# Gate products of 32 rows, two at a time on two groups of partitions, in a hybrid encoder trunk

## What is computed

```python
g_f = (jax.nn.log_sigmoid((a_f @ w2_f + b_f).astype(jnp.float32)) / GLA_TAU).reshape(B, S, GLA_HEADS, GLA_DK)
g_b = (jax.nn.log_sigmoid((a_b @ w2_b + b_b).astype(jnp.float32)) / GLA_TAU).reshape(B, S, GLA_HEADS, GLA_DK)
...
b = jnp.cumsum(gc, axis=2)
```

## Time and profile before

| | us |
|---|---|
| median of 3 runs | 2955.53 |
| fastest, slowest run | 2954.26, 2968.17 |
| the profiled execution's own time | 2966.03 |
| its span in the trace | 2964.2 |
| TensorE busy in it | 2886.0 |

### The profile page before, as it was taken

One profiled execution on the slowest core, in us unless ns is written; L12 is line 12 of the kernel. 1 busy time (PEld: TensorE's weight loads), 2 busy tenths in 40 slices (PEclk: granted clock), 3 DMA queues, 4 the chain that ended last, 5 costly groups with the idle time before them and its releaser, 6 DMA issues.

```text
span 2964.2 us, 48975 instructions
## 1 busy us (share of the span) xinstructions
PE 2886.0 (97%) x16038; PEld 2405.6 (81%) x16038; DVE 1605.5 (54%) x2745; ACT 1365.5 (46%) x2458; POOL 1143.6 (39%) x1118
## 2 busy tenths in 40 slices
PE   7999999999999999999999999999999999999998
PEld 6768888788788888887877888888887888888887
DVE  6577777766677777774435222254557554532111
ACT  4642255566555555553236111265657665632111
POOL 1211111356233333332331762087766767623221
PEclk9999999988999999999999999999999999999999
DMA  7243355586211111113653332242235233244321
GB/s 281 68 123 103 106 165 163 166 284 211 59 57 57 57 57 57 57 57 115 200 180 121 135 149 89 96 132 100 99 103 181 101 106 101 96 164 149 101 98 57
DMA packets 277929, 355.56 MB, mean 120 GB/s; under 512 B 21604, under 2 KB 185572, under 8 KB 277255
## 3 DMA queue, kind: packets, MB, share of 16 engines
q1 hardware_dynamic: 272424, 338.14, 35.0%
q0 software_dynamic: 3072, 11.54, 1.0%
q10 hardware_dynamic: 2304, 4.20, 0.4%
HBM read 241.99 MB, written 111.80 MB: 119 GB/s over the span
## 4 chain that ended last, share of the span: by engine, by line
PE 84%; DVE 4%; issue 4%; ACT 4%; POOL 2%; DMA 2%; SPq 0%; DVEq 0%; ACTq 0%; POOLq 0%
PE PS L3025 6%; PE PS L3029 6%; PE PS L3033 6%; PE PS L366 4%; PE PS L2384 4%; PE PS L2385 4%; PE PS L2386 4%; PE PS L368 4%; PE PS L367 4%; PE PS L1805 4%; PE PS L1783 4%; PE PS L2552 4%; PE PS L2553 3%; PE PS L2554 3%; PE PS L1806 2%
## 5 line engine op out<-in xcount | busy, mean ns | idle before, releaser
L366 PE MATMUL PS<-hTh,whi 128*128 128x512 f32 x640 | 257.8, 403 | 1.5 <-DVE hTl L320 1.1
L3025 PE MATMUL PS<-hTh,wc 128*128 128x512 f32 x896 | 244.3, 395 | 6.6 <-DVE zu L2959 5.0
L368 PE MATMUL PS<-hTh,wlo 128*128 128x512 f32 x640 | 250.5, 391 | 0.0
L367 PE MATMUL PS<-hTl,whi 128*128 128x512 f32 x640 | 250.3, 391 | 0.0
L2781 POOL TENSOR_TENSOR wc<-wpr,wc 128x512 fp32r<-128x512 f32 x128 | 177.1, 1383 | 180.9 <-ACT wc L2777 180.9
L1886 ACT ACTIVATE pb__160<-PS,nm,rq 128x512 f32<-128x512 f32 x256 | 197.3, 779 | 106.7 <-DVE nm L1949 106.5
L3029 PE MATMUL PS<-hTh,wc 128*128 128x512 f32 x896 | 240.4, 390 | 0.0
L3033 PE MATMUL PS<-hTl,wc 128*128 128x512 f32 x896 | 240.4, 390 | 0.0
L2384 PE MATMUL PS<-ow_h,of_h 128*128 128x512 f32 x576 | 224.4, 390 | 1.8 <-DVE oy L2335 1.8
L2386 PE MATMUL PS<-ow_h,of_l 128*128 128x512 f32 x576 | 224.1, 389 | 0.0
L2385 PE MATMUL PS<-ow_l,of_h 128*128 128x512 f32 x576 | 224.1, 389 | 0.0
(11 more groups left out here) (309 smaller groups left out, 7130.1 us busy)
## 6 DMA issues: line engine op xcount, KB each, us to landing
wpr<-wuz SPq DMA_DIRECT2D x128, 256.0 KB, 3.2
xt<-x SPq DMA_DIRECT2D x8, 2048.0 KB, 9.0
mw<-wmod SPq DMA_DIRECT2D x64, 256.0 KB, 2.7
oxt<-x SPq DMA_DIRECT2D x32, 512.0 KB, 4.6
sg_v<-vev SPq DMA_DIRECT2D x64, 256.0 KB, 2.4
vm<-sg_v SPq DMA_DIRECT2D x32, 512.0 KB, 3.9
sgT<-mT SPq DMA_DIRECT2D x32, 512.0 KB, 3.5
chnk<-pev SPq DMA_DIRECT2D x48, 256.0 KB, 2.7
```

The lines of the kernel that those rows point to most:

```text
L366: pe.matmul(PS[:, bank, :], w[1][:, s, k, :], hTh[:, k, b], start=(k == 0), stop=False)
L367: pe.matmul(PS[:, bank, :], w[1][:, s, k, :], hTl[:, k, b], start=False, stop=False)
L368: mm = pe.matmul(PS[:, bank, :], w[2][:, s, k, :], hTh[:, k, b], start=False, stop=(k == KD - 1))
L3025: pe.matmul(o, wc[:, k, 0, kk, :], h_tile(hTh, k, kk), start=(kk == 0 and not onto), stop=False, skip_group_check=onto)
```

## The change

The 32 rows of `ga` and `gw2` are now held on two groups of partitions, 0 to 31 and 32 to 63. `gw2` is loaded twice, once to each group. `ga` is split by the parity of the block of positions: even blocks (tb = 0 and 2) on the first group, odd ones (tb = 1 and 3) on the second, so that it has 64 partitions with half as many columns. The first product of a pair reads from the first group, the second from the second. Banks, sums, and all that follows are as before. Two more DMAs are waited for, so the counts go from 80 to 112.

```diff
-        ga = at("ga", X0 + 24 * K, [2 * RANK, S])
+        ga = at("ga", X0 + 24 * K, [4 * RANK, 2, 512])
+        GROUP = (slice(0, 2 * RANK), slice(2 * RANK, 4 * RANK))
...
-        gw2 = at("gw2", X0 + 38 * K, [2 * RANK, 4 * P])
+        gw2 = at("gw2", X0 + 38 * K, [4 * RANK, 4 * P])
...
-            for dst, src in ((gw2[:, :], a["w2"]), (gb2[:, :], a["b2"]), (ggn[:, :], a["gnorm"]),
+            for dst, src in ((gw2[GROUP[0], :], a["w2"]), (gw2[GROUP[1], :], a["w2"]), (gb2[:, :], a["b2"]), (ggn[:, :], a["gnorm"]),
                              (gmask[:, :], a["cst"][:, C_MASK:C_INVF])):
                 sp.dma_start(dst, src).then_inc(s_gc, 16)
             stored(sp, 6)
-            sp.dma_start(ga[:, :], projT[T_GA, 0:2 * RANK, :]).then_inc(s_gc, 16)
+            for u in range(2):
+                sp.dma_start(ga[GROUP[u], :, :], projT[T_GA, 0:2 * RANK, :].rearrange("r (b u c) -> u r b c", u=2, c=512)[u]
+                             ).then_inc(s_gc, 16)
...
-                pe.wait_ge(s_gc, 80)
+                pe.wait_ge(s_gc, 112)
...
-                pe.matmul(PS[:, 2 + 2 * (i % 2) + u, :], gw2[:, n * P:(n + 1) * P], ga[:, tb * 512:(tb + 1) * 512],
+                pe.matmul(PS[:, 2 + 2 * (i % 2) + u, :], gw2[GROUP[u], n * P:(n + 1) * P], ga[GROUP[u], tb // 2, :],
                           start=True, stop=True).then_inc(s_gl, 1)
...
-        s_pos, E_pos = s_gc, 80
+        s_pos, E_pos = s_gc, 112
```

## The result

The changed kernel takes 2964.89 us, median of 22 runs (2953.50 to 2970.86); the kernel before, in 22 runs beside them, 2956.30 us (2954.26 to 2968.17). The ratio is 1.002 with a 95% interval of 1.0011 to 1.0029: 0.2% slower, where 4 us less was forecast. The difference of the medians is 8.6 us. The ratios in this document are not the quotients of the medians (that would be 1.0029 here), so where the two differ, read the interval. The time lies inside the range, and within the 0.5% called no change; the sign was wrong. The profiled execution of the changed kernel took 2966.84 us, span 2965.2, and starts 0.65 us late: its block ahead of the first gate product ends that much later than before.

A forecast was written before the change was run, and what follows sets the result against it. The ScalarE and VectorE chain up to L677 was taken to bound the start of the level products, TensorE everything after. Gains of 1.25 + 2.6 = 3.9 us gave 2955.53 - 3.9 = 2951.6 us; range 2945 to 2966.

The forecast's parts named there:

- The overlap: Gate products on TensorE: both halves of a pair run side by side, 0.85 us a pair, 6.8 us in all; chance 0.60.
- half-overlap rival: Gate products: second product's first half runs beside the first's second half only, 0.43 us a pair; 2952.9 us, chance 0.22.
- drain: Gate products: changing rows drains the array, nothing overlaps, a turn is 8.0 us; about 2957.6 us, chance 0.10.
- no overlap: Gate products: a pair's two products don't overlap and nothing moves; 2955.5 us, chance 0.08.
- First split: GpSimd's first weight-tile split in the gate stage starts at 129.91, not 131.62; ScalarE and VectorE go on 1.1 us sooner.
- Second split: GpSimd's next weight-tile split starts at 156.8, not 161.94, amid pair 4's scans; ScalarE and VectorE then 1.25 us ahead.
- the chain: Gate stage: ScalarE's Abs, Exp, Ln, VectorE's subtraction L574, then the next pair's Abs; one turn is 7.48 us.
- Evictions and third split: Block 19 waits 2 us for an eviction; GpSimd splits from 183.7; first level distance loses 0.55, not 3.14: -2.6 us.
- DMAs: Two more loads issued by SyncE, about 0.47 us each, cost nothing; 0.9 us if the cover were gone.
- everything keeps its distance to it: After the level products start 3.9 us sooner, TensorE is the bound and the end comes 3.9 us sooner.
- the clock term: Half clock behind the idle time before the level products, a 2.8 us loss, left alone; bounds 2.8 us to either side.
- The 46 us at half speed: Stage from 590 to 780 us: mean granted clock 0.88, counted in the range as pieces that may fall otherwise.

The follow-up runs named there:

- loads_only: Kernel before with w2 loaded twice and ga in two loads, all products still on partitions 0 to 31; median 2955.67 us, ratio 1.0005.
- one_group: Changed kernel, but both products of a pair read the same partition group, so pairs don't overlap; median 2956.54 us, ratio 1.0003 to the kernel before.
- a_inpad: Changed kernel with 4 useless products behind every pair, restoring the old turn; median 2959.89 us, ratio 1.0010 to the kernel before.
- b_pad16: Kernel before with 16 useless products (3.4 us) behind the third level unit; median 2968.12 us, ratio 1.0024.
- b_less12: Kernel before without 12 of the 24 products of projection block 40, 2.7 us less work; median 2957.76 us, ratio 1.0001.
- warm2: Changed kernel with 24 and 20 useless products in TensorE's two longest waits behind the gates; median 2957.56 us, ratio 0.9998 to the kernel before.
- b_same: Kernel before, unchanged, run again; median 2959.59 us, ratio 1.0008.

## Why the prediction was wrong

- **The overlap: right.** Both halves of a pair run side by side: 1.13 us for 1.1, a turn of 6.72 for 6.73. In the trace a pair's first two records start 7 ns apart (116.902, 116.909), the second two as well (117.435, 117.442). The Trainium skill (TensorE: Matmul & The Clock Gate, Part 3, The mechanism) has matmuls start and end strictly in program order; the order is kept here, by 7 ns, and it doesn't keep a later product's first half behind an earlier one's second. The half-overlap rival, and drain and no overlap with it, are out.
- **First split: right.** With the 0.65 us off it starts at 129.91 (forecast 129.9); the fourth Abs is 1.48 us sooner, forecast 1.1.
- **Second split: wrong.** It starts at 156.79 as forecast (156.8), but the chain is then 0.1 us ahead, not 1.25. I let only the scans and the subtraction meet GpSimd. The two pairs of small operations between them met it too (158.56 and 160.35), and the subtraction queued behind them. That is 1.15 of the 1.4 us between a start of L699 2.5 us sooner and the forecast 3.9; the rest is the third split, which gave 2.4 us and not 2.6. The Trainium skill (SBUF — State Buffer, SBUF: two separate sides) says that whichever of VectorE and GpSimd has their shared ports holds them for the whole instruction; by that rule a tiny operation waits as long as a scan, and the trace agrees. It limits this to VectorE operations with two SBUF inputs, and then only against a GpSimd operation that reads SBUF (as the splits do), or in a mode of two ports; the small ones have one input, and no row tells their mode.
- **Evictions and third split: right in kind.** Waits of 1.40 and 1.74 us for L397 in place of one of 2; the split at 185.2 (with the 0.65 off) and not 183.7; the first level distance takes 1.03 us, a loss of 0.75 for the forecast 0.55, and all later ones 0.28. The idle time ahead of L699 stays, 6.75 us.
- **DMAs: right.** loads_only is no slower than the kernel before that its runs could show (1.0005, 0.9996 to 1.0014).
- **The step that failed** is "After that TensorE is the bound, and everything keeps its distance to it: 3.9 us at the end", with the clock term beside it left alone as equally likely to either side. TensorE is the bound, and its work kept its order and waits, but its rate did not stay. From 590 us on the low stretches fell elsewhere and were longer: against one_group the changed kernel's profile lost 8.1, 3.3 and 2.7 us in three places, and over all runs the mean granted clock fell from 0.9890 to 0.9857 and 0.9866. The 46 us at half speed that the prediction counted in the earlier trace rows was the sign of it: 0.88 is what the profiled execution had, 10.5 us over the median; one_group and a_inpad, at 2955 us each, have 0.94 and 0.95 there. So I moved the sum to a median whose executions already lie near the low end of what this term does; a shift of any kind had more room to lose than to gain, and b_pad16 and b_less12, each away from the timing of before, point that way: neither is faster, and both lose more clock than one_group in their profiles (29.8 and 29.3 us for 21.6).

**What stays open.** Shown: the loss is clock, by the profiles and by the mean clock of all runs, and it comes with the overlapping products and not with the DMAs or the partitions. Likely, but not certain: that it comes with the changed times and not with the overlap itself (a_inpad). Not shown: why these times are worse than those of before. No single distance that I read told long executions from short ones in all profiles, and each kernel has both. That the kernel before happens to sit at a good place is an inference from a few shifted kernels and the changed one.

The Trainium skill (TensorE: Matmul & The Clock Gate, Part 1, What's actually happening) says of the ramp at a kernel's start that it differs from run to run of one kernel and costs under 1% of a typical span, and not to fit to a particular count of slow products. The size here is of that order, though these stretches lie all over the kernel: 20.8 to 34.3 us in the six profiles of the kernel before, loads_only, one_group and the changed kernel, 0.7% to 1.2% of the span. The difference between them is larger than everything this change can give.

## What to carry to other kernels

Pack products of few rows onto different groups of rows if the pair's time is on the bound: they overlap fully, halves and all. But a gain of 0.1% can't be forecast, or credited to its edit, while the granted clock of later stages moves by more than that: read the clock by stage in several executions first, and take what the low clock cost off each span before comparing two kernels. Filling a wait with useless products keeps the clock up behind it, but its work counts: here it took the changed kernel's loss away (warm2) and gave the kernel before nothing that shows. And when a busy engine pair excludes each other, count every operation between two big ones, however small.

## What the runs showed of the hardware beyond that

- Profiles of one and the same kernel (before and b_same) lost 33.5 and 28.1 us to the lower clock, and without it their spans are 1.1 us apart (estimates from the traces). The time of this kernel, whose TensorE is busy for 97%, isn't the sum of its work to within some 0.3%, but nearly all of the scatter between its executions is clock.
- Float32 products of 32 rows on different row groups start 7 ns apart in both of their records, and two take 1.13 us, of which the first record's latency is part.
- After a wait of 6.75 us the granted clock is 0.50 for 10.2 us, though TensorE works again after 4.7 of them (in one_group's profile for 6.8); with products in the wait it is 1.00 throughout. After the same wait of 1.73 us and in the same one-column products it fell for 3.4 us in one execution and 6.8 in another.
- Pairs of VectorE operations on 4 columns, 0.24 us a pair elsewhere, took 1.75 and 2.44 us beside a GpSimd operation on 1024.
